# Means of seven norms from the high and low parts of the sums, and two of the last five stores on ScalarE's queue

## The reference

```python
def rmsnorm(x, g):
    xf = x.astype(jnp.float32)
    y = xf * lax.rsqrt(jnp.mean(xf * xf, axis=-1, keepdims=True) + EPS)
    return (y * g.astype(jnp.float32)).astype(x.dtype)

def layer_forward(x, p_i, norm_g, w1g, w1u, w1d, w2g, w2u, w2d, w_pe, w_pg, mix):
    x = x + 0.5 * swiglu(rmsnorm(x, norm_g[0]), w1g, w1u, w1d)
    y, st = mix(rmsnorm(x, norm_g[1]))
    x = x + y
    x = x + 0.5 * swiglu(rmsnorm(x, norm_g[2]), w2g, w2u, w2d)
    x = x + (p_i @ w_pe) * jax.nn.sigmoid(rmsnorm(x, norm_g[3]) @ w_pg)
    return x, st
```

## Time and profile before

| | |
|---|---|
| median of 3 runs | 1187.56 us (1187.52 to 1188.17) |
| profiled execution, its own time | 1188.66 us |
| its span, first to last instruction | 1186.9 us |
| granted TensorE clock over the span | 0.997 |
| busy: PE, DVE, ACT, POOL | 1171.9, 791.1, 583.6, 156.7 us |

### The profile page before, as it was taken

One profiled execution on the slowest core, in us unless ns is written; L12 is line 12 of the kernel. 1 busy time (PEld: TensorE's weight loads), 2 busy tenths in 40 slices (PEclk: granted clock), 3 DMA queues, 4 the chain that ended last, 5 costly groups with the idle time before them and its releaser, 6 DMA issues.

```text
span 1186.9 us, 23365 instructions
## 1 busy us (share of the span) xinstructions
PE 1171.9 (99%) x9004; PEld 1164.0 (98%) x9004; DVE 791.1 (67%) x1176; ACT 583.6 (49%) x861; POOL 156.7 (13%) x192
## 2 busy tenths in 40 slices
PE   9999999999999999999999999999999999999996
PEld 9999999999999999999999999999998999999996
DVE  6665555677778665565885665556989856655566
ACT  6444343566655444434664444335795544443353
POOL 0000011212231000011320000111307200000122
PEclk9999999999999999999999999999999999999998
DMA  6545444743355445344464444445444554444442
GB/s 240 183 171 176 141 150 156 271 135 107 107 177 189 149 169 177 133 163 152 156 212 170 154 171 144 147 171 187 144 163 133 192 181 150 173 155 143 174 152 90
DMA packets 37788, 193.22 MB, mean 163 GB/s; under 512 B 4160, under 2 KB 6352, under 8 KB 26208
## 3 DMA queue, kind: packets, MB, share of 16 engines
q1 hardware_dynamic: 36112, 186.81, 46.0%
q0 software_dynamic: 1040, 4.51, 1.2%
q10 hardware_dynamic: 576, 1.05, 0.3%
HBM read 188.78 MB, written 3.58 MB: 162 GB/s over the span
## 4 chain that ended last, share of the span: by engine, by line
PE 90%; DVE 5%; DMA 2%; ACT 2%; issue 0%; DVEq 0%; SPq 0%; ACTq 0%
PE bank L1215 29%; PE bank L1216 29%; PE bank L1217 29%; DVE w_lo L814 2%; PE bank L1254 1%; DVE conv L949 1%; DVE u_ext L962 1%; DMA raw<-in_lru_g 1%; DVE xg_lo L823 0%; DMA raw<-in_up 0%; ACT w_hi L535 0%; DMA raw<-in_lru_o 0%; DMA x_res<-in_x 0%; PE bank L1268 0%; PE bank L1238 0%
## 5 line engine op out<-in xcount | busy, mean ns | idle before, releaser
L535 ACT ACTIVATE w_hi<-raw 128x1024 fp32r<-128x1024 f32 (+2 forms) x410 | 370.6, 927 | 340.1 <-PE bank L1217 322.6
L814 DVE TENSOR_TENSOR w_lo<-raw,w_hi 128x1024 fp32r<-128x1024 f32 (+2 forms) x410 | 449.4, 1114 | 81.2 <-ACT w_hi L535 79.1
L1215 PE MATMUL bank<-xg_hi,w_hi 128*128 128x288 f32 x1536 | 455.9, 297 | 1.9 <-DVE w_lo L845 1.1
L1216 PE MATMUL bank<-xg_lo,w_hi 128*128 128x288 f32 x1536 | 452.9, 295 | 0.0
L1217 PE MATMUL bank<-xg_hi,w_lo 128*128 128x288 f32 x1536 | 450.4, 293 | 0.0
L1215 PEld LDWEIGHTS bank<-xg_hi,w_hi 128*128 128x128 f32 x1536 | 288.1, 188 | 3.5 <-issue 1.5
L1217 PEld LDWEIGHTS bank<-xg_hi,w_lo 128*128 128x128 f32 x1536 | 288.6, 188 | 0.0
L1216 PEld LDWEIGHTS bank<-xg_lo,w_hi 128*128 128x128 f32 x1536 | 288.0, 187 | 0.4
L1216 PE MATMUL bank<-h_lo,w_hi 128*128 128x288 f32 x704 | 208.7, 296 | 0.0
L1215 PE MATMUL bank<-h_hi,w_hi 128*128 128x288 f32 x704 | 207.3, 295 | 0.0
L1217 PE MATMUL bank<-h_hi,w_lo 128*128 128x288 f32 x704 | 207.2, 294 | 0.0
(11 more groups left out here) (193 smaller groups left out, 1272.7 us busy)
## 6 DMA issues: line engine op xcount, KB each, us to landing
raw<-in_up SPq DMA_DIRECT2D x85, 1024.0 KB, 4.8
raw<-in_down SPq DMA_DIRECT2D x64, 704.0 KB, 4.0
raw<-in_qkv SPq DMA_DIRECT2D x24, 512.0 KB, 4.7
raw<-in_ple SPq DMA_DIRECT2D x16, 640.0 KB, 3.8
raw<-in_lru_in SPq DMA_DIRECT2D x12, 512.0 KB, 4.5
raw<-in_lru_o SPq DMA_DIRECT2D x8, 640.0 KB, 3.9
raw<-in_wo SPq DMA_DIRECT2D x4, 1024.0 KB, 5.7
raw<-in_lru_g SPq DMA_DIRECT2D x8, 512.0 KB, 4.3
```

The source lines that it names most:

```text
L535: nc.scalar.activation(w_hi[slot][:, cols], raw[slot][:, cols], ACT.Copy).then_inc(w_hi_done, 1)
L814: nc.vector.tensor_tensor(w_lo[slot][:, cols], raw[slot][:, cols], w_hi[slot][:, cols].bitcast(F32), ALU.subtract).then_inc(w_lo_done, 1)
L1215: nc.tensor.matmul(out, w_hi[slot][:, cols], hi[:, k, 0:width], start=start, stop=False)
L1216: nc.tensor.matmul(out, w_hi[slot][:, cols], lo[:, k, 0:width], start=False, stop=False)
```

## The change

Stages 1 to 7 no longer hand `sum_squares` to a full-precision matmul. ScalarE copies the sums to `sums_hi` (fp32r), VectorE subtracts to get `sums_lo`, and TensorE multiplies both by `mean_r`, an fp32r matrix of 1/1024 (exact, a power of two), adding the two products in the same bank. TensorE waits for the new semaphore `sums_done`. Stage 0 and the final norm stay as they were. The second and fourth of the five last stores are issued from ScalarE. GpSimd sets one more matrix at the start.

```diff
 LAST_PIECES = ((0, 0, 4), (0, 4, 8), (1, 0, 4), (1, 4, 6), (1, 6, 8))
+
+OTHER_QUEUE = (1, 3)
...
             for n, (half, lo, hi) in enumerate(LAST_PIECES):
-                cols = TOKEN_HALVES[half]
-                sp.wait_ge(out_ready, n + 1)
-                sp.dma_start(a["y"][:, lo:hi, cols], y_rows[:, lo:hi, cols]).then_inc(y_stored, 16)
+                if n not in OTHER_QUEUE:
+                    cols = TOKEN_HALVES[half]
+                    sp.wait_ge(out_ready, n + 1)
+                    sp.dma_start(a["y"][:, lo:hi, cols], y_rows[:, lo:hi, cols]).then_inc(y_stored, 16)
...
+            nc.gpsimd.memset(mean_r[:].bitcast(F32), 1.0 / D_MODEL).then_inc(consts, 1)
...
+            def sums_high(stage):
+
+                act.wait_ge(summed_squares, (stage + 1) * KD)
+                nc.scalar.activation(sums_hi[:], sum_squares[:], ACT.Copy).then_inc(sums_hi_done, 1)
...
                     if n == 0 and turn is None and kind in ("up", "qkv", "ple", "lru_in"):
+                        if stage > 0:
+                            sums_high(stage)
                         root(stage)
...
+            for n in OTHER_QUEUE:
+                half, lo, hi = LAST_PIECES[n]
+                cols = TOKEN_HALVES[half]
+                act.wait_ge(out_ready, n + 1)
+                act.dma_start(a["y"][:, lo:hi, cols], y_rows[:, lo:hi, cols]).then_inc(y_stored, 16)
...
                     if n == 0 and turn is None and kind in ("up", "qkv", "ple", "lru_in"):
+                        if stage > 0:
+                            dve.wait_ge(sums_hi_done, stage)
+                            nc.vector.tensor_tensor(sums_lo[:], sum_squares[:], sums_hi[:].bitcast(F32), ALU.subtract) \
+                                .then_inc(sums_done, 1)
                         inverse(stage)
...
+                if stage > 0:
+                    pe.wait_ge(consts, 3)
+                    pe.wait_ge(sums_done, stage)
+                    nc.tensor.matmul(bank[7][:, 0:TOK], mean_r[:], sums_hi[:], start=True, stop=False)
+                    nc.tensor.matmul(bank[7][:, 0:TOK], mean_r[:], sums_lo[:], start=False, stop=True) \
+                        .then_inc(mean_done, 1)
+                    return
                 nc.tensor.matmul(bank[7][:, 0:TOK], mean_w[:], sum_squares[:], start=True, stop=True) \
                     .then_inc(mean_done, 1)
```

More of the change, by code:

```diff
@@ L218, in build @@
         mean_w = sb("mean_w", [P, P])
+        mean_r = sb("mean_r", [P, P], F32R)
+        sums_hi, sums_lo = sb("sums_hi", [P, TOK], F32R), sb("sums_lo", [P, TOK], F32R)
         fold = sb("fold", [P, QUARTER])
@@ L288, in build @@
         fold_made, diagonal_done, spread = sem("fold_made"), sem("diagonal_done"), sem("spread")
+        sums_hi_done, sums_done = sem("sums_hi_done"), sem("sums_done")
         consts, mean_done, std_done, rstd_done = sem("consts"), sem("mean_done"), sem("std_done"), sem("rstd_done")
```

## The result

The changed kernel took 1193.74 us (median of 6 runs, 1192.89 to 1194.99), the kernel before 1187.87 us beside it; the ratio is 1.0041 with a 95% interval of 1.0031 to 1.0051. It is slower, as forecast. The ratio is not the quotient of the two medians, which is 1.0049. The forecast of 4.1 us on 1187.56 is a ratio of 1.0035, inside that interval; the median itself lies 0.24 us above the upper end of the range. The profiled execution has a span of 1191.4 us, 4.5 us more than before.

A forecast was written before the change was run, and what follows sets the result against it. The prediction took PE, busy for 99% of the span, as the bound. Four stalls of 5.27 us less 1.17 us gained at seven means, stores 0, lose 4.10 us: 1187.56 + 4.10 = 1191.7 us, range 1189.8 to 1193.5 (8 in 10).

The forecast's parts named there:

- What bounds the kernel: Whole span: PE is busy for 99%, so what it loses in a phase is lost unless a later wait swallows it.
- Rival 2: Recurrent-block waits swallow up to 2.2 us of the stalls, or VectorE's splits run faster: 1189.5 us; chance 0.09.
- The mean: At each mean, two fp32r products take 0.26 us instead of 0.49: 0.23 us gained, 0.12 where PE stalls.
- Four spacings: At each mean, the skill's four passes for true fp32: 0.52 us, a gain of 0.26 us, sum below 0.2 lower.
- Which means stall: PE waits for VectorE's subtraction at `up1`, `ple0`, `up2`, `ple1`; not at `qkv`, `lru_in`, `up3` (0.20 us in hand).
- How long: Stalls of 1.43, 1.22, 1.40 and 1.22 us at `up1`, `ple0`, `up2`, `ple1`: 5.27 us.
- The step that failed: GpSimd's additional matrix is set in the first microseconds and first needed in stage 1: it costs nothing.
- the bound by which a short split at `up1` would take off 0.86 us: At `up1`, VectorE's split takes 3.44 us against 2.58 in `up3`; a short one would take off 0.86 us.
- The stores: At the end, transfer engines are full, so moving stores to ScalarE's queue gives 0, bounds -0.6 and +0.6 us.
- Rival 3: A stall drops the clock to 1.2 GHz, one `up` group takes 6.2 us more: 1197.9 us; chance 0.05.
- The sum: Whole kernel: 1187.56 + 4.10 = 1191.7 us; profiled span near 1191.0 us.

The follow-up runs named there:

- two fills more: Changed kernel with two more GpSimd fills of a 128x1 tile at the start; 1192.90 us, ratio 1.0034 to the kernel before.
- the fill alone: Kernel before with only one more GpSimd fill of an unused 128x128 matrix at the start; 1190.58 us, ratio 1.0015.
- the last experiment: Changed kernel plus two small fills, stores on SyncE, full-precision mean in `ple0` and `ple1`, mean of `up1` and `up2` four tiles later; 1187.83 us, ratio 0.9987.
- the stores: Kernel before with the second and fourth of the last five stores on ScalarE's queue and GpSimd's `mean_r` fill kept; 1190.77 us, ratio 1.0010.
- the norms: Changed kernel with all five last stores on SyncE's queue; 1194.84 us, ratio 1.0046 to the kernel before.
- the wait: Changed kernel still making and awaiting both parts of the sums, but with one full-precision product for the mean; 1196.78 us, ratio 1.0058 to the kernel before.
- the pair without the wait: Changed kernel with the fp32r products on constant-filled matrices, no high and low parts made or awaited; 1188.11 us, ratio 0.9991 to the kernel before.

## Why the prediction was right, point by point

**What bounds the kernel.** Right. The waits added to PE came out as time: in the ledger the lag behind `up2` is +4.06 us, at the end +4.5. Rival 2 falls, with a reserve for the recurrent block: there the lag fell by 1.15 us in the profile with two fills more, but it stayed within 0.02 us in that of the fill alone and fell by 0.91 us in that of the last experiment, where PE had no lag to lose. So it is not the stall that is swallowed; what moves the recurrent block is open. The faster split that rival 2 names did come at `up1`, and saved nothing (below).

**The mean.** Right. 0.23 us gained at each free mean (forecast 0.23). At the stalled ones the pair takes 0.21 + 0.13 = 0.34 us (forecast 0.37). Four spacings in place of the measured 0.49 us would have moved the sum by 7 x 0.03 = 0.21 us, a little more than the prediction's "below 0.2".

**Which means stall.** Right for all seven, with `up3` 0.26 us in hand from the end of the subtraction to PE's start.

**How long.** From the time at which PE was due (0.13 us after the product ahead) to the pair's start it is 2.31, 1.32, 1.49 and 1.32 us at `up1`, `ple0`, `up2` and `ple1`: 6.44 us, forecast 5.27. Two terms were too small. PE follows the subtraction after 0.15 us, not 0.05: the row that the prediction took, a product that waited for `y_lo`, is not a mean's; why the two differ was not tried. That is 0.1 us at each of the four. The rest, 0.8 us, is `up1`. Of its 2.31 us, 0.66 us are there because PE was due that much sooner (363.35, against 364.01 before) and could not use it: 0.30 us of lead stem from `qkv` and the start, 0.36 us from the groups between. The pair itself was ready at 365.66, only 0.22 us later than forecast, but by another path: the prediction had VectorE's place as the limit, and the sums themselves ended last.

**The step that failed** is the sentence that GpSimd's additional fill costs nothing. With that one fill in, in five kernels of five (the changed one, the stores, the norms, the wait, the fill alone), the gap ahead of the next square in GpSimd's loop for `up1`, where it waits for nothing, is 0.26 us; with none, or with three, in five of five, it is 0.18. The 0.08 us matter because VectorE starts its split 0.24 us after GpSimd's last addition ends, in all ten traces: with the longer gap GpSimd's square comes after VectorE's instruction has begun, and takes 1.72 us instead of 0.67. The Trainium skill ("SBUF — State Buffer", section SBUF: two separate sides) says that a VectorE instruction with two inputs in SBUF, as the split is, and a GpSimd instruction that reads SBUF share a pair of ports as an exclusive lock: the one that starts first has it for the whole instruction, and the other blocks. The trace agrees, since the order of the two decides which of them is stretched: in the kernels with the short gap GpSimd's square takes 0.67 us and VectorE's split 3.44 us, in those with the long gap 1.72 and 2.82 (where the split stands in one piece). This also answers the bound by which a short split at `up1` would take off 0.86 us: the split was 0.62 us shorter, but by the same event that made the sums late, and nothing was gained. What the fill cost shows against the changed kernel with two fills more: from ahead of `qkv` to behind the mean of `up1` PE loses 1.49 us with one fill and 0.94 with three. Why one fill lengthens the loop's step and three do not is open. The place of the tiles in memory is not the reason, since the pair without the wait has the same tiles as the changed kernel and the short gap; that the instructions of the loop come to lie elsewhere is only argued.

**The stores.** Right: no gain and no loss, 6.57 us of tail against 6.59.

**The clock.** Rival 3 was given 0.05 and was half true. The clock did fall after the stall at `up1`, in the profiles of the norms alone and of the wait alone, and not there in those of the changed kernel, with the same stall, and of the kernel with two fills more (stall of 1.49 us); the price was 1.56 and 1.54 us, not the 6.2 that a whole group would have cost. The prediction's ground against it was that the shorter waits of the recurrent block had left the clock alone. That was so in the one profile it had, and does not hold: in five profiles of ten, the changed kernel's among them, the clock stood at 0.50 behind those waits for 3.4 us (three) or 6.8 us (two). From `lru_in` to `up3` PE's lag changed by -0.20 to +0.04 us in the three, by +1.55 and +2.13 in the two, and by -1.15 to -0.02 in the four other profiles without a fall. So the whole span of one profile is not to be read closer than 1 to 2 us, and the experiments are read at the means. How often the clock falls in unprofiled runs was not measured. The six runs of the changed kernel lie in two groups, at 1192.9 to 1193.2 us with a mean clock of 0.996 to 0.997 and at 1194.3 to 1195.0 with 0.994 to 0.995, which such falls would explain, at either place; the kernel before, without the new stalls, has a similar spread among its 28 runs (1188.1 to 1189.1 us at 0.997, 1190.5 and 1191.3 at 0.993).

**The sum.** Two errors partly met: the stalls were 1.2 us longer, and 0.6 us came back between the means. They are not independent, since 0.36 us of what came back is the lead that PE then lost again at `up1`. And it is in part luck that the span came within 0.4 us of its forecast of 1191.0, as the recurrent block alone can move it by more.

## What to carry to other kernels

A cheaper instruction on the engine that bounds the kernel is only worth its saving if what feeds it is ready when that engine arrives; a preparation step on another engine must be costed at its place in that engine's program, behind everything queued ahead of it, and not by its own length. Where it comes late, move the step forward or the use of it back: five of the seven pairs, put where VectorE comes first, turned +0.4% into -0.13%. And look at the timeline of an engine whose program has gained even one instruction at the start before counting it as free.

## What the runs showed of the hardware that was not expected

One more fill of 128x128 on GpSimd in the first microsecond lengthened the steps of one loop of the same engine, hundreds of microseconds later, by 0.08 us (gap 0.18 to 0.26, ahead of `up1`), and two further fills undid it; in the loop ahead of `up3` the gap is 0.18 us in all ten kernels. Through the order in which GpSimd and VectorE then met, the 0.08 us became 0.6 us in the sums of `up1` (364.55 against 363.94), and a wait of 1.1 us on TensorE in a kernel that was otherwise unchanged, whose ratio was 1.0015. A stall of TensorE of 2.2 us in the middle of dense work was followed, in two profiles of three, by a fall of the granted clock to its 1.2 GHz level for 3.4 us, at a price of 1.5 to 1.6 us; three or four waits of up to 0.9 us in the recurrent block were followed by such a fall in five profiles of ten.
